# First MLP's down projection as a stream of seven block products over 16 inner tiles

## The chip, the cores and the metric

One Trainium2 chip; the program runs on one core. The metric is the device time in microseconds (us), lower is better. TensorE (PE) multiplies, VectorE (DVE), ScalarE (ACT) and GpSimd (POOL) work element by element, and SyncE (SP) issues the transfers from one queue, in which a wait holds back everything behind it.

## What is computed

Three transformer blocks follow one another on an activation x of 1024 rows and 1024 features, in 32-bit floats. The change lies in the MLP of the first block and touches that of the third:

```python
hn = rms_norm(h, norm_mlp_w)                                     # first block
h = h + jnp.square(jax.nn.relu(hn @ w_up)) @ w_down              # 1024 -> 4096 -> 1024
...
mod = jax.nn.silu(c) @ w_ada + b_ada                             # third block: 6 x 1024 values
...
h = rms_norm_3(x, norm2_pre) * (1.0 + scale2) + shift2
f = jnp.square(jax.nn.relu(h @ w_fc1)) @ w_fc2                   # 1024 -> 4096 -> 1024
x = x + gate2 * rms_norm_3(f, norm2_post)
```

`mod` needs only the input `c`, so the kernel computes it during the first block's MLP.

## The kernel before

**Precision.** Every 32-bit matmul is three: each operand is split into a rounded high part and a low part (the rest), and high x high, high x low and low x high are accumulated in PSUM. ScalarE makes the high parts (a copy into the rounded type), GpSimd or VectorE the low parts (a subtraction). A product of a 128x128 weight tile and a 128x512 half of an activation tile is thus three matmuls of 512 columns.

**Layout.** Activations are transposed: X holds 8 tiles of 128 features by 1024 rows. The 4096 hidden features are 32 inner tiles. While an MLP's up projection runs (`fast_all`, a seven-product scheme over 2x2 blocks, parts p1, p5, p6, p4, p7, p2, p3 in this order for each pair of tiles), each finished hidden tile is spilled to `hsc` in device memory, and is loaded again later.

**First MLP's down before.** 40 jobs `dn{g}_{m}`: five groups g of 8, 4, 4, 8 and 8 inner tiles, and in each group the 8 output tiles m. A job over 8 inner tiles is 48 matmuls, one over 4 is 24. Its result stands in a PSUM bank and VectorE adds it to X (`to_x`). The first three groups, jobs 0 to 23, cover inner tiles 0 to 15 with 8 x 2 x 3 x 16 = 768 matmuls. Beside the jobs VectorE forms the 48 rows of `w_ada` needed for `mod` (`row_step`, list `ADAS`): eight products of 128x128 with a column of silu(c), added up in PSUM, for each row tile; TensorE then reduces each with one short matmul (`row`, L1062) two jobs later. Their loads (`row_load`) stand in SyncE's queue.

**Third MLP's down before.** Inner tiles 0 to 23 go as a stream of seven products of blocks (`blocks`, `BLOCKS`): the output is cut in 2x2 quarters (4 output tiles by 512 rows), the inner dimension in two halves of `NK` = 12 tiles. A block takes 12 steps, one for each inner tile k of a half; a step is 4 output tiles x 3 = 12 matmuls (L842 to L844). Seven blocks do the work of eight. In the first two and the last two steps of a block TensorE takes output tiles 0 and 1 of both steps before tiles 2 and 3 (`BORDER`), so that finished banks come in two halves. For step s:

- SyncE loads weights for two steps at a time (`weight_load`, v = s // 2, four places; 512 KB for each weight block that the product needs, one or two), as soon as step 2v - 7, the last that used the place, is done, and then half tiles of the hidden activation (`block_load`, 256 KB). Quarters of it are named (half of the inner dimension, half of the rows): (0,0), (1,0), (1,1), (0,1).
- ScalarE: `block_copy(s + 1)` copies one half tile into PSUM (L1632), then `block_highs(s)` rounds the activation (L1641) and the weights (L1643) of step s.
- VectorE: adds or subtracts the second half tile where the block needs a sum, then makes the low part of step s - 1. For some steps it also adds two weight blocks. At steps 3 and 4 of the next block it adds the finished products to X (`block_out`); ScalarE does this for outputs that are written first.
- GpSimd: `block_sum(s + 1)` adds weight blocks (where VectorE doesn't), then the low part of the weights of step s.

ScalarE, VectorE and GpSimd can be at most four steps ahead of TensorE, since there are four places for the rounded activation. The order in `block_step` of ScalarE, and in that of VectorE before:

```python
if s + 1 < NSTEP:
    block_copy(s + 1)          # ScalarE
block_highs(s)
...
if sum_on_vector(s + 1):       # VectorE: s // NK == 2 or s in (3, 5, 7, 9, 11)
    tt(wblock(s + 1, 0), wblock(s + 1, 0), wblock(s + 1, 1), ADD, f"S sW {s + 1}")
block_sum(s)
block_low(s - 1)
```

The stream begins right behind the up projection. In SyncE's queue stood, before: weight load 0; then half tiles 0 to 3, weight load 1, half tiles 4 to 11, weight loads 2 and 3 (load 2 waits for the last parts of the up projection, load 3 for step 1), the spills of hidden tiles 31 and 30, and weight load 4, which waits for spill 31 to land.

The functions that the diff touches:

Of the kernel before, what the change touches and what calls it, by code (L numbers as in the profile page):

```python
# [16 lines left out]
P = 128  # L17
# [6 lines left out]
ADAS = [[0]] + [[2 * n - 1, 2 * n] for n in range(1, 9)] + [[n + 8] for n in range(9, 24)] + [[2 * n - 16, 2 * n - 15] for n in range(24, 32)] + [[]] * 8  # L24
assert sum(ADAS, []) == list(range(48))
# [19 lines left out]
NK = 12  # L45
NSTEP = len(BLOCKS) * NK
BORDER = ([(k, j) for a in (0, 2) for k in (0, 1) for j in (a, a + 1)] + [(k, j) for k in range(2, NK - 2) for j in range(4)]
          + [(k, j) for a in (0, 2) for k in (NK - 2, NK - 1) for j in (a, a + 1)])
WPLACE = [0, 1, 2, 0] + [(3, 1, 2, 0)[v % 4] for v in range(4, 36)] + [3, 1, 2, 3, 1, 2]


def sum_on_vector(s):

    return s // NK == 2 or s in (3, 5, 7, 9, 11)

# [13 lines left out]
SPLIT = ("dn0_0", "fdn0_0")  # L69
# [93 lines left out]
def stream(d):  # L163
# [13 lines left out]
    def phases(up, dn, t):  # L177
        for f in range(2 * NQ[t]):
            plan(tile_name(t, f), d[up][NQ[t] * (f % 2) + f // 2 if t == "fup" else f])
        for g, z in enumerate(SZ[t]):  # L180
            if t == "fa1_" and g < 4:
# [96 lines left out]
def build(nc, d, out):  # L278
    ctx = ExitStack()
    with ctx:  # L280
# [176 lines left out]
        AR = [T[1], RT, T[2]]  # L457
# [6 lines left out]
        BU = {(0, 0): [GF[:, k // 2, half(k % 2)] for k in range(NK)], (1, 0): [GXF[:, k // 2, half(k % 2)] for k in range(NK)],  # L464
              (1, 1): [HXF[:, k, half(1)] for k in range(4, 8)] + [HF[:, k, half(1)] for k in (4, 5, 6, 7, 0, 1, 2, 3)],
              (0, 1): [HXF[:, k, half(0)] for k in range(4, 8)] + [HF[:, k, half(0)] for k in range(4, 8)] + [HXF[:, k, half(1)] for k in range(4)]}
        wplace = (WO, TO + 4096, WO + 8192, RO)
        WF = [at(f"WF{i}", a, [P, 2048]) for i, a in enumerate(wplace)]
        WR = [at(f"WR{i}", a, [P, 2048], R) for i, a in enumerate(wplace)]
# [3748 lines left out]
```

## Time and profile before

| | us |
|---|---|
| median of 3 runs | 3313.03 (3308.84 to 3313.93) |
| profiled execution | 3316.2, its span 3314.2 |
| TensorE busy | 3255.0 |
| first MLP's down, 40 jobs | 795.73 to 1157.01 |
| of it groups 0 to 2 | 795.73 to 978.29 |
| third MLP's stream, 84 steps | 2975.72 to about 3211 |

Times in the profile count from the span's start. TensorE's matmuls overlap: the length given for one (389 ns for 512 columns) is longer than the distance to the next. The clock column is TensorE's granted clock, 1.00 being 2.4 GHz and 0.50 being 1.2 GHz.

### The profile page before, as it was taken

Reading aid. Unit: us, or ns where it says so; the run is one execution under the profiler, and the core shown is the slowest. Engines: PE = TensorE matmul, PEld = TensorE weight load, DVE = VectorE, ACT = ScalarE, POOL = GpSimd, SP = SyncE. Lnnn points to the kernel's source line nnn. Section 1 sums busy time; section 2 is a strip of 40 time slices with the busy share of each in tenths; the row PEclk is TensorE's granted clock in tenths of the full one; section 3 lists DMA queues with packets and bytes.
Section 4 is the critical chain, followed back from the end, with each engine's and each line's share of the span. In section 5 each row is a group of like instructions: output and inputs, shape, how many; then the busy total and the mean of one; then the engine's idle time right before and its main releaser. Section 6 shows DMA issues by size and latency. Waiting matters only on the chain.

```text
span 3314.2 us, 40211 instructions
## 1 busy us (share of the span) xinstructions
PE 3255.0 (98%) x16118; PEld 2648.4 (80%) x16118; DVE 2008.5 (61%) x2966; ACT 1299.0 (39%) x2014; POOL 1288.5 (39%) x768
## 2 busy tenths in 40 slices
PE   8999999999999999998999999999999999999998
PEld 6788888888888878875687888888888888887887
DVE  4563347665564538577558888776536485655553
ACT  5332233333121221176535545521223364456652
POOL 3112324555353213231424554554212215555963
PEclk9999999999999999999999999999999999999999
DMA  3011312235554212111022222366111132247743
GB/s 111 31 58 65 127 51 96 110 117 191 177 206 165 96 39 70 57 66 42 5 98 70 77 82 90 107 230 231 58 59 45 39 133 108 110 158 241 238 149 121
DMA packets 142502, 358.36 MB, mean 108 GB/s; under 512 B 15958, under 2 KB 58726, under 8 KB 142188
## 3 DMA queue, kind: packets, MB, share of 16 engines
q1 hardware_dynamic: 142316, 355.79, 30.8%
q8 instruction: 128, 2.10, 0.3%
q14 instruction: 58, 0.48, 0.1%
HBM read 292.66 MB, written 63.09 MB: 107 GB/s over the span
## 4 chain that ended last, share of the span: by engine, by line
PE 90%; DVE 5%; ACT 2%; DMA 1%; POOL 1%; issue 0%; SPq 0%; POOLq 0%; DVEq 0%; ACTq 0%
PE ps L751 16%; PE ps L752 16%; PE ps L754 16%; PE ps L809 9%; PE ps L811 9%; PE ps L810 9%; PE ps L842 2%; PE ps L843 2%; PE ps L844 2%; PE ps L993 1%; PE ps L1216 1%; PE ps L784 1%; PE ps L786 1%; PE ps L785 1%; PE ps L1265 1%; PE ps L1249 1%
## 5 line engine op out<-in xcount | busy, mean ns | idle before, releaser
L3512 POOL TENSOR_TENSOR wlo<-raw,whi 128x1024 fp32r<-128x1024 f32 (+3 forms) x162 | 388.6, 2399 | 1174.8 <-ACT whi L1499 1174.8
L751 PE MATMUL ps<-HH,whi 128*128 128x512 f32 (+2 forms) x1520 | 607.1, 399 | 2.3 <-DVE HL L2358 1.4
L752 PE MATMUL ps<-HL,whi 128*128 128x512 f32 (+2 forms) x1520 | 597.1, 393 | 0.0
L1499 ACT ACTIVATE whi<-raw 128x1024 fp32r<-128x1024 f32 (+3 forms) x164 | 163.2, 996 | 817.3 <-PE ps L754 789.6
L754 PE MATMUL ps<-HH,wlo 128*128 128x512 f32 (+2 forms) x1536 | 476.6, 392 | 0.0
L3582 POOL TENSOR_TENSOR wlo<-raw,whi 128x512 fp32r<-128x512 f32 x188 | 275.0, 1464 | 281.4 <-ACT whi L1596 240.2
L754 PEld LDWEIGHTS ps<-HH,wlo 128*128 128x128 f32 (+2 forms) x1536 | 287.3, 187 | 66.0 <-issue 1.1
L751 PEld LDWEIGHTS ps<-HH,whi 128*128 128x128 f32 (+2 forms) x1520 | 285.0, 188 | 67.0 <-issue 3.0
L752 PEld LDWEIGHTS ps<-HL,whi 128*128 128x128 f32 (+2 forms) x1520 | 284.9, 187 | 61.9 <-issue 2.0
L2342 DVE TENSOR_TENSOR T<-T,ps 128x512 f32<-128x512 f32 (+1 forms) x254 | 174.3, 699 | 231.1 <-PE ps L811 192.4
L2342 DVE TENSOR_TENSOR X<-ps,X 128x1024 f32<-128x1024 f32 (+1 forms) x91 | 108.1, 1188 | 313.9 <-PE ps L754 296.8
L751 PE MATMUL ps<-GH,whi 128*128 128x512 f32 x752 | 295.8, 393 | 0.8 <-POOL wlo L3512 0.6
L809 PE MATMUL ps<-OHp,whi 128*128 128x512 f32 x752 | 292.7, 389 | 0.9 <-POOL wlo L3582 0.9
L752 PE MATMUL ps<-GL,whi 128*128 128x512 f32 x752 | 292.8, 389 | 0.0
L810 PE MATMUL ps<-OLp,whi 128*128 128x512 f32 x752 | 292.6, 389 | 0.0
L754 PE MATMUL ps<-GH,wlo 128*128 128x512 f32 x784 | 241.6, 389 | 0.0
L809 PE MATMUL ps<-HH,whi 128*128 128x512 f32 x564 | 219.6, 389 | 1.6 <-POOL wlo L3582 1.6
L810 PE MATMUL ps<-HL,whi 128*128 128x512 f32 x564 | 219.4, 389 | 0.0
L1596 ACT ACTIVATE whi<-raw 128x512 fp32r<-128x512 f32 x188 | 118.0, 628 | 193.4 <-PE ps L811 187.9
L754 PEld LDWEIGHTS ps<-GH,wlo 128*128 128x128 f32 x784 | 147.2, 188 | 31.1
L3582 POOL TENSOR_TENSOR HH<-HXF,whi 128x512 fp32r<-128x512 f32 x93 | 121.9, 1311 | 113.6 <-ACT whi L1596 60.1
L809 PEld LDWEIGHTS ps<-OHp,whi 128*128 128x128 f32 x752 | 141.2, 188 | 30.8 <-POOL wlo L3582 1.6
(514 smaller groups left out, 6624.8 us busy)
## 6 DMA issues: line engine op xcount, KB each, us to landing
raw<-in_w_up SPq DMA_DIRECT2D x76, 512.0 KB, 4.1
WF<-in_w_fc SPq DMA_DIRECT2D x72, 512.0 KB, 4.5
raw<-in_w_in SPq DMA_DIRECT2D x62, 512.0 KB, 3.3
hsc<-T SPq DMA_DIRECT2D x62, 512.0 KB, 2.7
GF<-hsc SPq DMA_DIRECT2D x42, 512.0 KB, 5.8
raw<-in_w_down SPq DMA_DIRECT2D x40, 512.0 KB, 5.3
raw<-in_w_fc SPq DMA_DIRECT2D x40, 512.0 KB, 4.0
T<-in_w_ada SPq DMA_DIRECT2D x32, 512.0 KB, 3.8
```

Of the source, the lines that this page charges most:

```text
L751: e.matmul(o_[0:m, half(hf)], whi_[k], hi[k0 + k][:, half(hf)], start=first, stop=False)
L752: e.matmul(o_[0:m, half(hf)], whi_[k], lo[k0 + k][:, half(hf)], start=False, stop=False)
L754: i = e.matmul(o_[0:m, half(hf)], wlo_[k], hi[k0 + k][:, half(hf)], start=False, stop=last)
L809: e.matmul(bank[p], wh[:, blk(k)], hi, start=k == 0 and p not in ("p2", "p7", "p3"), stop=False, skip_group_check=True)
L810: e.matmul(bank[p], wh[:, blk(k)], lo, start=False, stop=False, skip_group_check=True)
L811: i = e.matmul(bank[p], wl_[:, blk(k)], hi, start=False, stop=k == 3, skip_group_check=True)
L842: e.matmul(o_, wh, hi, start=k == 0, stop=False, skip_group_check=True)
L1499: e.activation(whi_of(name), v3(raw_of(name), 2) if name in SPLIT else raw_of(name), ACT.Copy).then_inc(*ac.inc("hi " + name))
L1596: e.activation(wh_of(t, w), part(t, n, p)[0], ACT.Copy).then_inc(*ac.inc(f"{t}hi {n} {p}"))
L2342: e.tensor_tensor(o, a, b, op).then_inc(*dv.inc(*names))
L3512: e.tensor_tensor(wlo_of(name), raw_of(name), whi_of(name).bitcast(F), SUB).then_inc(*po.inc("lo " + name))
L3582: e.tensor_tensor(o, x, wh_of(t, w).bitcast(F), SUB).then_inc(*po.inc(f"{t}lo {n} {p}"))
```

## The change

The first MLP's inner tiles 0 to 15 go as a stream too: seven blocks of 8 steps, 672 matmuls, in place of jobs 0 to 23. Jobs 24 to 39 (groups 3 and 4) stay; job 24 takes its inner tiles in the order 4 to 7, 0 to 3. `NK`, `NSTEP`, `BORDER`, `WPLACE` become tables by MLP ("up" is the first, "fa1_" the third); the first has a fifth weight place. Its stream order in SyncE's queue is `blocks1`: quarter (1,0) from weight load 5 on, (1,1) from 9 on, (0,1) from 21 on. In it all outputs are added to X by VectorE. A weight place is two separate halves.

In both streams VectorE adds the weight blocks of every odd step above 4 in blocks that have two, and does so after the low part of step s - 1 and not before the sum of step s. At the stream's start weight loads 1, 2, 3 stand behind half tiles 1, 3 and 5. In the third MLP half tiles 8 to 11 of quarter (0,0) come behind weight loads 3 and 4, quarter (1,0) comes with weight loads 7 to 12 (before: 3 to 8) and quarter (1,1) with 13 to 18 (before: 9 to 14).

The 48 rows become 12 groups of four (`ROWQ`), formed at jobs 24 to 32, 34, 36 and 38: eight products of 512 columns each, from four tiles of 512 KB (from group 9 on two tiles are free, and the second half of a group is loaded when the first has been used). The up projection takes its PSUM banks in the same order in both MLPs.

```diff
-ADAS = [[0]] + [[2 * n - 1, 2 * n] for n in range(1, 9)] + [[n + 8] for n in range(9, 24)] + [[2 * n - 16, 2 * n - 15] for n in range(24, 32)] + [[]] * 8
+ROWQ = {24 + n: n for n in range(9)} | {34: 9, 36: 10, 38: 11}
...
-NK = 12
+NK = {"up": 8, "fa1_": 12}
+G0 = {"up": 3, "fa1_": 4, "fup": 0}
+WPLACE = {"up": [0, 4, 2, 0] + [(1, 3, 2, 0)[v % 4] for v in range(4, 27)] + [1],
+          "fa1_": [0, 1, 2, 0] + [(3, 1, 2, 0)[v % 4] for v in range(4, 36)] + [3, 1, 2, 3, 1, 2]}
...
-def sum_on_vector(s):
-    return s // NK == 2 or s in (3, 5, 7, 9, 11)
+def sum_on_vector(t, s):
+    b = s // NK[t]
+    return BLOCKS[b][1] is not None and s % 2 == 1 and s > 4
...
             fast_all("up")
-            for n in range(40):
+            blocks("up")
+            for n in range(24, 40):
...
-            def block_step(s):
-                if sum_on_vector(s + 1):
-                    q.wait_ge(*wload_of(s + 1))
-                    tt(wblock(s + 1, 0), wblock(s + 1, 0), wblock(s + 1, 1), ADD, f"S sW {s + 1}")
-                if s < NSTEP:
-                    block_sum(s)
+            def block_step(t, s):
+                if s < NSTEP[t]:
+                    block_sum(t, s)
                 if s:
-                    block_low(s - 1)
-                if s > NK and s % NK in (3, 4):
-                    block_out(s // NK - 1, s % NK - 3)
+                    block_low(t, s - 1)
+                if s + 1 < NSTEP[t] and sum_on_vector(t, s + 1):
+                    q.wait_ge(*wload_of(t, s + 1))
+                    tt(wblock(t, s + 1, 0), wblock(t, s + 1, 0), wblock(t, s + 1, 1), ADD if BLOCKS[(s + 1) // NK[t]][2] > 0 else SUB, f"{t}S sW {s + 1}")
+                if s > NK[t] and s % NK[t] in (3, 4):
+                    block_out(t, s // NK[t] - 1, s % NK[t] - 3)
...
+            def blocks1():
+                for v in range(3, NSTEP["up"] // 2):
+                    if v == 27:
+                        loads(widx["dn3_1"])
+                    if v > 3:
+                        weight_load("up", v)
+                    for k in (2 * (v - 5) % 8, 2 * (v - 5) % 8 + 1):
+                        if 4 < v < 9:
+                            block_load("up", 1, 0, k, pe("up15 p4"))
+                        elif 8 < v < 13:
+                            block_load("up", 1, 1, k, pe("up15 p7"))
+                        elif 20 < v < 25:
+                            block_load("up", 0, 1, k, pe("upS 3"))
...
-                    for k in (2 * (v - 3) % NK, 2 * (v - 3) % NK + 1):
-                        if v < 9:
-                            block_load(1, 0, k, pe("fa1_15 p7"), ac(f"S cp {k}"))
-                        elif v < 15:
-                            block_load(1, 1, k, pe("fa1_15 p3"), dv(f"S sT {NK + k}"), *([spilled("fa1_", 30)] if k > 9 else []))
+                    if v in (3, 4):
+                        for k in (2 * v + 2, 2 * v + 3):
+                            block_load("fa1_", 0, 0, k, pe("fa1_15 p6"))
+                    for k in (2 * (v - 7) % 12, 2 * (v - 7) % 12 + 1):
+                        if 6 < v < 13:
+                            block_load("fa1_", 1, 0, k, pe("fa1_15 p7"), ac(f"fa1_S cp {k}"))
+                        elif 12 < v < 19:
+                            block_load("fa1_", 1, 1, k, pe("fa1_15 p3"), dv(f"fa1_S sT {12 + k}"), *([spilled("fa1_", 30)] if k > 9 else []))
...
-                    if (t, n) == ("fa1_", z):
-                        for k in range(4):
-                            block_load(0, 0, k, pe("fa1_15 p5"))
-                        weight_load(1)
-                        for k in range(4, NK):
-                            block_load(0, 0, k, pe("fa1_15 p5" if k < 8 else "fa1_15 p6"))
-                        weight_load(2)
-                        weight_load(3)
+                    if t in NK and n == z:
+                        for k in range(8):
+                            block_load(t, 0, 0, k, pe(f"{t}15 p5"))
+                            if k in (1, 3, 5):
+                                weight_load(t, (k + 1) // 2)
```

## Rows read from the trace of the kernel before

**Rows 1.** The page: busy time of the engines, and one costly group of VectorE.
```profile
PE 3255.0 (98%) x16118; PEld 2648.4 (80%) x16118; DVE 2008.5 (61%) x2966; ACT 1299.0 (39%) x2014; POOL 1288.5 (39%) x768
...
L2342 DVE TENSOR_TENSOR T<-T,ps 128x512 f32<-128x512 f32 (+1 forms) x254 | 174.3, 699 | 231.1 <-PE ps L811 192.4
```

**Rows 2.** Timeline of TensorE, first matmuls of stream blocks 1 and 2 (start, length).
```profile
3014.37 0.39 PE L842 MATMUL ps<-HH,WR 128*128 128x512 f32 x1
...
3047.01 0.39 PE L842 MATMUL ps<-HH,WR 128*128 128x512 f32 x1
```

**Rows 3.** Timeline of TensorE, first MLP's down: start, end of group 2, end.
```profile
795.73 0.39 PE L751 MATMUL ps<-GH,HH 128*128 128x512 f32 x1
...
978.15 0.28 PE L1062 MATMUL ps<-ones,adat 128*128 128x1 f32 x2
...
978.29 0.48 PE L751 MATMUL ps<-HH,whi 128*128 128x512 f32 x1
...
1157.01 0.39 PE L751 MATMUL ps<-HH,whi 128*128 128x512 f32 x1
```

**Rows 4.** Timeline of TensorE, third MLP's stream; bracketed: idle time and its end.
```profile
2975.72 0.39 PE L842 MATMUL ps<-HH,WR 128*128 128x512 f32 x1
...
2985.42 0.47 PE L842 MATMUL ps<-HH,WR 128*128 128x512 f32 x1 [1.22 <-POOL WR L3518]
...
2999.05 0.47 PE L842 MATMUL ps<-HH,WR 128*128 128x512 f32 x1 [2.44 <-POOL WR L3518]
...
3003.48 0.39 PE L842 MATMUL ps<-HH,WR 128*128 128x512 f32 x1
...
3050.36 0.47 PE L842 MATMUL ps<-HH,WR 128*128 128x512 f32 x1 [0.46 <-ACT ps L1632]
```

**Rows 5.** Windows: length, busy time by engine, granted clock, DMA share, GB/s.
```profile
2999.00:3003.40 4.40, 4.36 (x12) 3.47 (x13) 1.48 (x3) 2.75 (x6) 3.71 (x3) 0.61 1.00 358
...
3145.60:3178.20 32.60, 32.60 (x145) 27.00 (x145) 23.95 (x35) 23.51 (x42) 29.60 (x21) 1.00 0.78 266
```

**Rows 6.** Timeline of SyncE's queue, the last spills of the third MLP.
```profile
2982.47 0.50 SPq L3744 DMA_DIRECT2D hsc<-T  x1
...
2984.21 0.53 SPq L3744 DMA_DIRECT2D hsc<-HF  x1
```

**Rows 7.** DMA issues, windows from 2982.4, 2984.1, 3014.5, 3041.7, 3124: us to landing.
```profile
hsc<-T SPq DMA_DIRECT2D x1, 512.0 KB, 6.5
...
hsc<-HF SPq DMA_DIRECT2D x1, 512.0 KB, 5.9
...
HXF<-hsc SPq DMA_DIRECT2D x2, 256.0 KB, 4.4
...
HF<-hsc SPq DMA_DIRECT2D x2, 256.0 KB, 5.3
...
HF<-hsc SPq DMA_DIRECT2D x2, 256.0 KB, 6.4
```

**Rows 8.** Timeline of SyncE's queue, two weight loads in block 1.
```profile
3041.76 0.94 SPq L3744 DMA_DIRECT2D WF<-in_w_fc  x2
```

**Rows 9.** Timelines of ScalarE (copy) and GpSimd (low part), third MLP's block 1.
```profile
3045.42 0.60 ACT L1632 ACTIVATE ps<-HXF 128x512 f32<-128x512 f32 x1 [0.36 <-DVE HL L2342]
...
3047.17 1.30 POOL L3518 TENSOR_TENSOR WR<-WF,WR 128x512 fp32r<-128x512 f32 x1 [0.74 <-ACT WR L1643]
```

**Rows 10.** Timelines of GpSimd and VectorE, weight sums that met the other's work.
```profile
2982.24 1.81 POOL L3518 TENSOR_TENSOR WF<-WF 128x512 f32<-128x512 f32 x1 [3.53 <-DMA WF<-in_w_fc]
...
3047.32 1.70 DVE L2342 TENSOR_TENSOR WF<-WF 128x512 f32<-128x512 f32 x1 [1.99 <-DMA WF<-in_w_fc]
```

**Rows 11.** Timeline of VectorE, outputs of block 4 into X.
```profile
3145.80 2.47 DVE L2342 TENSOR_TENSOR X<-X,ps 128x512 f32<-128x512 f32 x4
```

**Rows 12.** Timeline of VectorE, norm low parts at the end of the first MLP.
```profile
1147.59 3.42 DVE L2358 SCALAR_TENSOR_TENSOR HL<-X,gprod,HH 128x1024 fp32r<-128x1024 f32 x1
...
1162.12 1.28 DVE L2358 SCALAR_TENSOR_TENSOR HL<-X,gprod,HH 128x1024 fp32r<-128x1024 f32 x1
```

More of the change, by code:

```diff
@@ L1064, in row_step @@
             def row_step(n):
-                for f in rows.pop(0):
-                    if f == 0:
-                        q.wait_ge(*ac("n2 rt"))
-                    q.wait_ge(*dv(f"red ada{f}"))
-                    row(f)
-                rows.append(ADAS[n] if n >= 0 else [])
+                for g in rows.pop(0):
+                    for f in range(4 * g, 4 * g + 4):
+                        q.wait_ge(*dv(f"red ada{f}"))
+                        row(f)
+                rows.append([ROWQ[n]] if n in ROWQ else [])
             def norm2(k):
@@ L2319, in scalar @@
             fast_all("fa1_", bias7)
-            for s in range(4, NSTEP):
-                block_step(s)
             for n in range(32, 40):
@@ L3606, in fast_all @@
                 for w in range(m):
-                    if w == m - 3 and t != "fa1_":
+                    if w == m - 3 and t not in NK:
                         lows(following(t, -1))
                     fast_lo(t, w)
-                if t == "fa1_":
-                    block_sum(0)
-                    for s in range(NSTEP):
-                        block_step(s)
+                if t in NK:
+                    block_sum(t, 0)
+                    for s in range(NSTEP[t]):
+                        block_step(t, s)
                     return
@@ L3631, in gpsimd @@
             fast_all("up")
-            for n in range(40):
+            for k in (0, 2):
+                low(f"dnl {16 + k}", GXF[:, k, :], HH[:, k, :], HL[:, k, :], ac(f"dnh {16 + k}"))
+            for n in range(24, 40):
                 down("up", n)
@@ L3872, in blocks @@
-            def blocks():
-                for v in range(3, NSTEP // 2):
+                f = k + NK[t] * l
+                q.wait_ge(*spilled(t, f))
+                load(f"hr{k}", BU[t][l, h][k], hsc[f][:, half(h)], f"{t}S{l}{h} {k}")
+            def blocks1():
[11 more added lines that the diff above has]
+                            block_load("up", 0, 1, k, pe("upS 3"))
+                    if 12 < v < 17:
+                        k = v - 9
+                        q.wait_ge(*pe("up15 p3"))
+                        q.wait_ge(*spilled("up", 16 + k))
+                        load(f"hr{8 + k}", HF[:, k, :], hsc[16 + k], f"uphr {16 + k}")
+                    elif v > 23:
+                        k = v - 24
+                        q.wait_ge(*dv(f"upS sT {4 * NK['up'] - 1}"))
+                        q.wait_ge(*spilled("up", 16 + k))
+                        load(f"hr{8 + k}", GXF[:, k, :], hsc[16 + k], f"uphr {16 + k}")
@@ L3875, in blocks, with blocks3 @@
+            def blocks3():
+                for v in range(3, NSTEP["fa1_"] // 2):
                     if v == 41:
```

433 lines of the change are left out of this document (238 added, 195 removed).

## The prediction, made before the changed kernel was run

> **What bounds the kernel now.** The page first. TensorE is busy for 98% of the span [rows 1]. So two things can move the time: how many matmuls there are, and how long TensorE stands still or runs slowly between them. The page's mean of a matmul, 389 ns, is not its price, because matmuls overlap. The timeline gives the price: block 1 of the third MLP's stream is 144 matmuls from 3014.37 to 3047.01 us, so 0.2267 us each [rows 2]. A step of a stream (one inner tile, 12 matmuls) is then 2.72 us and a block of eight steps 21.8 us.
>
> Next the stage that is replaced. The first MLP's down runs from 795.73 to 1157.01, and its first 24 tiles, 768 matmuls, end at 978.29 [rows 3]. They take 182.6 us, of which 768 x 0.2267 = 174.1 are matmuls; the remaining 8.5 are the 30 rows of the modulation vector that are reduced there, about 0.25 us each (0.14 to the next matmul, 978.15 to 978.29, which is itself 0.09 longer [rows 3]), and 1 us of short gaps.
>
> Then the stage that already works in the new way. The third MLP's stream starts at 2975.72. It has three stalls: 1.22 us of idle before 2985.42 and 2.44 before 2999.05, both until GpSimd had made a low part of weights, and 0.46 before 3050.36 [rows 4]. After the second TensorE's granted clock is 0.61 of full in 2999.0 to 3003.4, a mix of 1.2 and 2.4 GHz [rows 5]: 12 matmuls take 3003.48 - 2999.05 = 4.43 us for 2.72, so the drop costs 1.7 us [rows 4]. The idle of 1.22 us had none. The end of block 4 shows none: 32.60 busy of 32.60 us [rows 5].
>
> **The change, part by part.**
> (1) Fewer matmuls. 7 blocks x 8 steps x 12 = 672 for 768: 96 x 0.2267 = 21.8 us off. The 1 us of gaps goes too. The 48 rows stay, four at a time, at the same price. Gain 22.8.
>
> (2) The start of the new stream. Count from its first matmul; step n starts at 2.72 n. In a block's first and last two steps output tiles 0 and 1 come first, so a block's last step begins half a step early: step 7 needs its operands at 6.5 x 2.72 = 17.7. The queue waits for step 1 (5.4), then issues two weight loads, two half tiles (now put behind them) and the last two spills, by about 8.1. It then waits for spill 30 before weight load 4. In the third MLP spill 30 was issued at 2984.21 and took 5.9 us, to 2990.1, 14.4 after its stream's start; spill 31, of 0.5 MB like it, landed 1.1 us before, at 2988.97 [rows 6, 7]. Here 0.5 MB more is ahead, so 1.1 us, but the spill is issued a little earlier: I take 15. Then come two single loads and the first half tile of quarter (1,0), issued at 16.1; such a tile lands in 4.4 us behind one weight load [rows 7], 5 behind two: 21. VectorE sums that tile for step 8 before it makes the low part of step 7 (0.70 us each [rows 1]), so step 7 starts at 22.4: 4.7 us late. Bounds: 2 (the spill too lands in 4.4) and 7 (two more transfers' worth of queue).
>
> (3) The tiles of quarter (1,1), and of (0,1) in the first MLP, are now loaded four steps ahead. The pair for steps 2v-2 and 2v-1 is issued once step 2v-7 is done, behind two weight loads. ScalarE copies tile 2v-2 BEFORE it rounds tile and weights of step 2v-3, so step 2v-3 is behind the transfer. From the end of 2v-7 to the start of 2v-3 there are three steps, 8.2 us. The chain: the first weight load is issued at 3041.76, two steps before 3047.01 and so 0.2 after the end of its step, the second is out at 3042.70 and the tile follows [rows 2, 8], 1.2; landing 5.3 (median of that pair [rows 7]), 6.5; copy, rounding, rounding and GpSimd's low part, 3045.42 to 3048.47 [rows 9], 3.1. With the hand-off it is 9.6, so 1.4 us of stall. For the pair that opens a block, step 2v-3 is the last of the block before and begins half a step early: 2.8. A stall delays the next pair's loads just as much, so only every second pair adds one. Block 2 of the first MLP: 2.8 + 1.4 = 4.2. Block 5, whose (0,1) is copied in the same way: 4.2. Block 2 of the third, six pairs: 2.8 + 1.4 + 1.4 = 5.6, where before the loads were issued eight steps earlier and only the 0.6 at 3050.36 was lost: 5.0 net. Quarter (1,0) goes through VectorE and is behind a single weight load: 0.6 + 4.4 + 1.5 = 6.5 us, in time. Together 13.4; bounds 0 (landing under 3.9 us) and 21 (landing 6.4 us, as one pair did [rows 7], 1.1 us for each of the seven stalls).
>
> (4) The third MLP's start. Weight load 2 no longer stands behind twelve half tiles, so the 1.22 us goes. But load 4 decides, and it waits for spill 31, issued at 2982.47 and landed 6.5 us later [rows 6, 7]; two half tiles are now ahead of it, 1.1 us. 1.1 later in all; bounds -3 (2999.05's stall goes) and +3.
>
> (5) The clock. Four stalls here are of about 2.6 us or more (the start, the two openings of block 2, that of block 5), as long as the 2.44 that was followed by half speed. I charge 1.7 us for three of them: 5.1. Bounds 0 and 7. The Trainium skill (TensorE: Matmul & The Clock Gate, The HAM clock gate) says that the full clock is granted to activity and withdrawn for its lack; by that rule all four would be charged, 6.8.
>
> (6) Weight sums. Every second one goes to VectorE, in the third MLP 28 of 60 for 17. GpSimd had two operations of 1.3 us in a step of 2.72 [rows 9] and kept up, so nothing is gained at TensorE. A sum met by a GpSimd operation costs both: GpSimd 1.81 for 1.30 [rows 9, 10], VectorE 1.70 for 0.70 [rows 1, 10]. Two steps of GpSimd are then at most 3 x 1.3 + 0.5 = 4.4 of 5.44. The new order on VectorE (low part before the sum) removes a wait behind a weight load. 0; bounds -0.6 and the first rival. The Trainium skill (SBUF — State Buffer, SBUF: two separate sides) calls the pair of ports these engines share a lock held for the whole instruction; rows 10 agree, and the sum stays.
>
> (7) Block ends. VectorE alone adds the products into X here, at worst four half tiles in 2.47 us after each half of a block [rows 11]. The bank that they free is wanted one step into the next block; in the third MLP block 4 has this worst case and TensorE does not wait [rows 5]. 0.
>
> (8) Rows beside groups 3 and 4. Per tile VectorE has 1.2 us for X and eight products of 512 wide, about 0.65 each: 6.4 of 11.8. From row group 9 only two tiles are free, so half of each group is loaded while VectorE waits, some 4 us. In tile 38 that makes 9.5, and the two following norm operations, one of which takes 3.42 beside GpSimd [rows 12], end 2.7 to 4.7 us into what was idle time. The last low part was done at 1163.4, 6.4 after the last down tile [rows 3, 12]; gg0 needs it at 9.5. 1.0; bounds 0 and 4.
>
> **Sum.** -22.8 + 4.7 + 13.4 + 1.1 + 5.1 + 1.0 = +2.5 us on the profiled execution (3316.2 us, span 3314.2). The median of the runs shown is 3313.0; from it I get 3315.5, so 3316.
>
> **The rivals.** 0.2% is 6.6 us; less cannot be told from no change here.
> A, as summed, within 6.6 us either way: 0.44.
> B, slower: VectorE becomes the bound of the first MLP's stream. Point of decision: 21.8 us of work in a block of eight. It has sixteen tile operations at a spacing of 2.47 / 4 = 0.62 us [rows 11], 9.9; outputs 4.9; four weight sums at 0.70, 2.8, or at 1.70, 6.8. That is 17.6 or 21.6, before any hand-off between it and ScalarE. If the hand-offs add 1.7 us to the latter, 1.5 us is lost in each of six blocks, 9 us in all; with the charges of A, 2.5, it is 3325. For it: VectorE reads two SBUF operands while GpSimd works for more than half of the time. Against: at the worst block end of the third MLP nothing waited, though no weight sum lay there. 0.27 with larger stalls in (2) and (3).
> C, faster: the transfers are hidden. If the tiles of (3) land in under 3.9 us, or the engines run further ahead than I think, (3) and two clock charges go: -22.8 + 4.7 + 1.7 + 1.1 + 1.0 = -14.3, 3299. For it: behind one weight load a tile lands in 4.4. Against: behind two it took 5.3 and 6.4 [rows 7]. If half of the gain comes, 3306. 0.29.
>
> **How the numbers follow.** Faster 0.29, same 0.44, slower 0.27. A alone is 3306 to 3320. The range runs from C's full gain, 3299, to B with one more clock charge, 3328.
>
> **What would show it.** In the changed profile: 672 matmuls on the block lines before the first MLP's last two groups; a stall of about 5 us near step 7 there, ended by VectorE's low part behind a landing of GXF; in both streams, at the end of block 1 and at step 3 of block 2, idle of 1 to 3 us ended by GpSimd's low part, with ScalarE's copy waiting for a transfer; stretches at 1.2 GHz behind them; no stall in the last 16 down tiles. Wrong would be: copies that never wait for transfers (C), or VectorE without idle time from one block end to the next (B).

## The result and the profile after

The changed kernel takes 3323.93 us (median of 6 runs, 3318.79 to 3326.22). The kernel before, run beside it, takes 3311.51 (6 runs, 3305.77 to 3313.93). The ratio is 1.0035, with a 95% interval of 1.0023 to 1.0047: slower by 12 us. That is inside the predicted range of 3299 to 3328 and 8 above the predicted 3316. The profiled execution took 3323.6 us, its span is 3321.8. That is 7.6 more than the span before. The profiled execution before was itself 4.7 us above the median of its runs, so 7.6 and 12 don't contradict each other.

The page of the changed kernel, busy time of the engines:

```profile
PE 3246.0 (98%) x16022; PEld 2633.1 (79%) x16022; DVE 2058.9 (62%) x2839; ACT 1354.8 (41%) x2142; POOL 1302.3 (39%) x795
```

The 96 matmuls are gone (16118 in [rows 1], 16022 here) and yet the time is longer. TensorE's timeline in the first MLP's stream (start, length; in brackets the idle time ahead and what ended it):

```profile
794.85 0.39 PE L855 MATMUL ps<-HH,WR 128*128 128x512 f32 x1
...
810.23 0.47 PE L855 MATMUL ps<-HH,WR 128*128 128x512 f32 x1 [1.60 <-POOL WR L3547]
...
818.23 0.80 PE L855 MATMUL ps<-HH,WR 128*128 128x512 f32 x1 [3.63 <-DVE HL L2357]
...
845.50 0.47 PE L855 MATMUL ps<-HH,WR 128*128 128x512 f32 x1 [2.65 <-POOL WR L3547]
...
853.19 0.47 PE L855 MATMUL ps<-HH,WR 128*128 128x512 f32 x1 [0.63 <-DVE X L2357]
...
917.17 0.47 PE L855 MATMUL ps<-HH,WR 128*128 128x512 f32 x1 [2.38 <-POOL WR L3547]
...
925.69 0.47 PE L855 MATMUL ps<-HH,WR 128*128 128x512 f32 x1 [1.31 <-DVE X L2357]
...
949.28 0.47 PE L855 MATMUL ps<-HH,WR 128*128 128x512 f32 x1 [0.87 <-DVE HL L2357]
...
969.80 0.39 PE L764 MATMUL ps<-HH,whi 128*128 128x512 f32 x1
```

The stream takes 969.80 - 794.85 = 174.95 us. Its 672 matmuls at 0.2267 are 152.3, so 22.6 are lost. In the text below a stall is the delay of the next matmul against 0.2267 us of spacing; it is some 0.15 longer than the idle time in the bracket (1.75 for 1.60). The losses by place: 1.75 and 3.79 at the start and 2.5 of half speed behind them; 2.82 and 2.54 at the last step of blocks 1 and 4, where blocks 2 and 5 are about to open; 7.3 in eleven smaller stalls (0.79, 0.43, 0.52, 0.62, 0.80, 1.47, 0.43, 0.28, 0.30, 0.61, 1.03), seven of them ended by VectorE, two by GpSimd and two too short for a name; 1.9 in gaps too small to list. The 16 tiles behind it, with all 48 rows, run from 969.80 to 1155.32. From its start to there the first MLP's down takes 360.5 us, where it took 361.3 from its start to the same point [rows 3]. So of the 22.8 us that the missing matmuls and gaps were to give, 22.6 are lost again inside the stream.

TensorE's timeline in the third MLP's stream:

```profile
2974.16 0.39 PE L855 MATMUL ps<-HH,WR 128*128 128x512 f32 x1
...
2986.64 0.47 PE L855 MATMUL ps<-HH,WR 128*128 128x512 f32 x1 [1.44 <-POOL WR L3547]
...
2997.63 0.51 PE L855 MATMUL ps<-HH,WR 128*128 128x512 f32 x1 [2.55 <-POOL WR L3547]
...
3016.98 0.47 PE L855 MATMUL ps<-HH,WR 128*128 128x512 f32 x1 [1.14 <-DVE X L2725]
...
3045.88 0.76 PE L855 MATMUL ps<-HH,WR 128*128 128x512 f32 x1 [2.71 <-POOL WR L3547]
...
3061.02 0.47 PE L855 MATMUL ps<-HH,WR 128*128 128x512 f32 x1 [1.09 <-POOL WR L3547]
...
3218.51 0.39 PE L764 MATMUL ps<-GH,whi 128*128 128x512 f32 x1
```

That is 244.35 us, where the kernel before took 235.2 (2975.72 [rows 4] to 3210.94): 9.1 more. Where block 2 opens there was a stall of 0.6 [rows 4]; now there is one of 2.87 at the last step of block 1 (3045.88) and, at steps 3 and 7 of block 2, 1.25 and 1.20. The stalls at the start are nearly those of before. A stall of 1.30 one step into block 1 (3016.98) is new: TensorE wants a bank of block 0 back, whose output VectorE writes (line 2725). The two traces agree elsewhere: the first stream starts 0.9 us earlier, the first MLP's down is 0.8 shorter, from there to the third stream it is 0.1 longer, and behind the third stream it is the same. -0.9 - 0.8 + 0.1 + 9.1 is 7.5, the 7.6 of the span within rounding.

How the first stream starts, on SyncE's queue:

```profile
802.49 0.91 SPq L3781 DMA_DIRECT2D hsc<-T  x2
810.24 0.94 SPq L3781 DMA_DIRECT2D WF<-in_w_down  x2
811.22 0.97 SPq L3781 DMA_DIRECT2D GXF<-hsc  x2
```

and on VectorE:

```profile
816.88 0.70 DVE L2357 TENSOR_TENSOR ps<-GXF,ps 128x512 f32<-128x512 f32 x1 [5.65 <-DMA GXF<-hsc]
817.49 0.68 DVE L2357 TENSOR_TENSOR HL<-ps,HH 128x512 fp32r<-128x512 f32 x1
```

The last spills go out at 802.49 and land 6.9 us later. Weight load 4 follows at 810.24, the half tiles of (1,0) stand behind it, and VectorE waits 5.65 us for the first before it makes the low part that TensorE needs at 818.23. This is the mechanism of step (2) of the prediction; TensorE starts 23.4 us behind the stream's start, where 22.4 was expected.

How block 2 opens there. SyncE's queue, ScalarE (copy, rounding of tile, rounding of weights) and GpSimd:

```profile
836.02 0.94 SPq L3781 DMA_DIRECT2D WF<-in_w_down  x2
837.00 0.98 SPq L3781 DMA_DIRECT2D GXF<-hsc  x2
```

```profile
842.37 0.60 ACT L1648 ACTIVATE ps<-GXF 128x512 f32<-128x512 f32 x1 [2.66 <-DMA GXF<-hsc]
842.91 0.58 ACT L1657 ACTIVATE HH<-ps 128x512 fp32r<-128x512 f32 x1
843.39 0.62 ACT L1659 ACTIVATE WR<-WF 128x512 fp32r<-128x512 f32 x1
...
847.65 0.60 ACT L1648 ACTIVATE ps<-GXF 128x512 f32<-128x512 f32 x1 [1.60 <-DMA GXF<-hsc]
```

```profile
844.08 1.27 POOL L3547 TENSOR_TENSOR WR<-WF,WR 128x512 fp32r<-128x512 f32 x1 [1.75 <-ACT WR L1659]
```

From the first weight load to TensorE are 845.50 - 836.02 = 9.5 us; the prediction had 9.6. And what the prediction did not follow, VectorE in the same place:

```profile
844.20 1.70 DVE L2357 TENSOR_TENSOR WF<-WF,WF 128x512 f32<-128x512 f32 x1
...
848.91 0.69 DVE L2357 TENSOR_TENSOR HL<-ps,HH 128x512 fp32r<-128x512 f32 x1 [2.24 <-ACT HH L1657]
849.52 1.73 DVE L2357 TENSOR_TENSOR WF<-WF,WF 128x512 f32<-128x512 f32 x1
851.17 0.68 DVE L2357 TENSOR_TENSOR HL<-ps,HH 128x512 fp32r<-128x512 f32 x1
851.77 2.47 DVE L2357 TENSOR_TENSOR X<-ps,X 128x512 f32<-128x512 f32 x4
```

The outputs of block 1 (851.77) free a bank that TensorE wants. They stand in VectorE's order behind the low part of 848.91, which waits 2.24 us for ScalarE, which waits at 847.65 for the next late tile; and behind a weight sum of 1.73. TensorE waits for them at 853.19.

TensorE's clock behind five stalls (windows: length, PE busy, granted clock, DMA share, GB/s):

```profile
818.80:824.20 5.40, 5.40 (x15) 0.55 0.06 20
845.50:849.70 4.20, 4.20 (x19) 1.00 0.50 176
917.20:921.30 4.10, 4.10 (x18) 1.00 0.58 201
2997.60:3002.00 4.40, 4.37 (x12) 0.61 0.56 194
3045.90:3050.00 4.10, 4.10 (x12) 0.61 0.49 172
```

### The profile page after: what moved, and what is told of

It is laid out like the page before. It is cut to its first block, busy times and chain, and to the rows that moved or that the text cites. A ratio compares the mean times of both kernels' runs of the same rounds, so it can differ in the third digit from the quotient of the medians.

```text
span 3321.8 us, 40243 instructions
## 1 busy us (share of the span) xinstructions
PE 3246.0 (98%) x16022; PEld 2633.1 (79%) x16022; DVE 2058.9 (62%) x2839; ACT 1354.8 (41%) x2142; POOL 1302.3 (39%) x795
## 4 chain that ended last, share of the span: by engine, by line
PE 88%; DVE 6%; ACT 2%; DMA 2%; POOL 1%; issue 1%; SPq 0%; POOLq 0%; DVEq 0%; ACTq 0%
PE ps L764 14%; PE ps L765 14%; PE ps L767 14%; PE ps L822 9%; PE ps L824 9%; PE ps L823 9%; PE ps L855 3%; PE ps L857 3%; PE ps L856 3%; PE ps L1007 1%; PE ps L1230 1%; PE ps L797 1%; PE ps L799 1%; PE ps L798 1%; PE ps L1279 1%
## 5 line engine op out<-in xcount | busy, mean ns | idle before, releaser
L3541 POOL TENSOR_TENSOR wlo<-raw,whi 128x1024 fp32r<-128x1024 f32 (+3 forms) x139 | 353.3, 2542 | 1081.0 <-ACT whi L1515 1081.0
L764 PE MATMUL ps<-HH,whi 128*128 128x512 f32 (+2 forms) x1456 | 581.1, 399 | 2.3 <-DVE HL L2373 1.4
L767 PE MATMUL ps<-HH,wlo 128*128 128x512 f32 (+1 forms) x1472 | 457.5, 392 | 0.0
L767 PEld LDWEIGHTS ps<-HH,wlo 128*128 128x128 f32 (+1 forms) x1472 | 275.1, 187 | 63.2 <-issue 1.1
L2357 DVE TENSOR_TENSOR T<-T,ps 128x512 f32<-128x512 f32 (+1 forms) x254 | 174.2, 699 | 228.8 <-PE ps L824 190.0
L855 PE MATMUL ps<-HH,WR 128*128 128x512 f32 x560 | 222.7, 398 | 25.9 <-POOL WR L3547 16.6
L3547 POOL TENSOR_TENSOR WR<-WF,WR 128x512 fp32r<-128x512 f32 x140 | 191.2, 1369 | 137.1 <-ACT WR L1659 137.0
L2357 DVE TENSOR_TENSOR X<-ps,X 128x512 f32<-128x512 f32 (+1 forms) x135 | 121.5, 924 | 194.6 <-PE ps L767 170.5
L764 PE MATMUL ps<-GH,whi 128*128 128x512 f32 x576 | 226.1, 393 | 0.6 <-POOL wlo L3541 0.6
L765 PE MATMUL ps<-GL,whi 128*128 128x512 f32 x576 | 224.2, 389 | 0.0
L857 PE MATMUL ps<-HH,WR 128*128 128x512 f32 x560 | 220.3, 393 | 0.0
L856 PE MATMUL ps<-HL,WR 128*128 128x512 f32 x560 | 220.2, 393 | 0.0
```

Source lines behind the costliest of these rows:

```text
L764: e.matmul(o_[0:m, half(hf)], whi_[k], hi[k0 + k][:, half(hf)], start=first, stop=False)
L765: e.matmul(o_[0:m, half(hf)], whi_[k], lo[k0 + k][:, half(hf)], start=False, stop=False)
L767: i = e.matmul(o_[0:m, half(hf)], wlo_[k], hi[k0 + k][:, half(hf)], start=False, stop=last)
L855: e.matmul(o_, wh, hi, start=k == 0, stop=False, skip_group_check=True)
L856: e.matmul(o_, wh, lo, start=False, stop=False, skip_group_check=True)
L857: i_ = e.matmul(o_, wl_, hi, start=False, stop=k == NK[t] - 1, skip_group_check=True)
```

## The experiments

The totals of the twelve kernels move with the other 2,900 us too: the first stream began anywhere between 789.3 and 799.0 us in them. So each is read by the length of the two streams in its trace, with the ratio of its time to the kernel before as a check. A stream's length goes from its first matmul to the first one of what follows; there is one trace of each kernel. Where two kernels have the same code for a stream, it differs by up to 0.7 us in the first MLP (e3 and e6) and by up to 1.9 in the third (243.3 to 245.2 in the kernels with the changed one's loads), so differences of that size are no effect by themselves. Theory 1 is the prediction's: late transfers, with ScalarE's copy queued ahead of its roundings. Theory 2: VectorE, with weight sums and all outputs, is what the stream waits for.

| run | first stream | third stream | median us | ratio to before (95%) |
|---|---|---|---|---|
| before | none | 235.2 | 3311.5 | 1 |
| after | 175.0 | 244.4 | 3323.9 | 1.0035 (1.0023 to 1.0047) |
| e1 | 174.2 | 233.1 | 3311.4 | 0.9998 (0.9989 to 1.0008) |
| e2 | 171.2 | 240.7 | 3314.9 | 1.0005 (0.9996 to 1.0015) |
| e3 | 162.3 | 243.9 | 3310.1 | 0.9990 (0.9980 to 1.0000) |
| e4 | 172.1 | 243.9 | 3319.2 | 1.0022 (1.0012 to 1.0031) |
| e5 | 168.6 | 243.3 | 3318.5 | 1.0020 (1.0010 to 1.0030) |
| e6 | 161.6 | 234.5 | 3297.3 | 0.9967 (0.9954 to 0.9979) |
| e7 | 154.4 | 232.2 | 3286.7 | 0.9932 (0.9919 to 0.9946) |
| e8 | 161.1 | 231.8 | 3298.5 | 0.9970 (0.9959 to 0.9982) |
| e9 | 153.3 | 231.9 | 3286.3 | 0.9929 (0.9915 to 0.9942) |
| e10 | 155.2 | 233.1 | 3288.3 | 0.9937 (0.9923 to 0.9952) |
| e11 | 161.5 | 245.2 | 3309.2 | 0.9993 (0.9982 to 1.0003) |
| e12 | 153.6 | 231.9 | 3287.8 | 0.9934 (0.9920 to 0.9948) |

Some of the expectations below give lengths 0.2 to 0.5 us shorter than this table (161.8 for e3's first stream); they were read from or to a neighbouring matmul. The kernel before was run again beside each group of kernels (medians 3311.5, 3310.8, 3308.6 and 3311.9), and each ratio is against its own group.

**e1, the third MLP's loads as they were.**

```diff
-if v in (3, 4): ... block_load("fa1_", 0, 0, k, ...)
-for k in (2 * (v - 7) % 12, 2 * (v - 7) % 12 + 1):
-    if 6 < v < 13:    block_load("fa1_", 1, 0, k, ...)
-    elif 12 < v < 19: block_load("fa1_", 1, 1, k, ...)
+for k in (2 * (v - 3) % 12, 2 * (v - 3) % 12 + 1):
+    if v < 9:    block_load("fa1_", 1, 0, k, ...)
+    elif v < 15: block_load("fa1_", 1, 1, k, ...)
...
+if (t, n) == ("fa1_", z):   # all twelve half tiles of (0,0) first, as in the kernel before
+    for k in range(12):
+        block_load(t, 0, 0, k, ...)
+        if k == 3:
+            weight_load(t, 1)
+    weight_load(t, 2)
+    weight_load(t, 3)
```

> The changed kernel, with the loads of the third MLP's stream in the order of the kernel before (its quarters (1,0) and (1,1) from step pair 3 and 9 on, four pairs earlier, and all twelve half tiles of (0,0) ahead of weight load 2). The changed kernel's third stream took 244.3 us, 235.4 before. Theory 1 (late transfers in front of ScalarE's copy): the stalls of 2.87, 1.25 and 1.20 us at the opening of block 2 and behind it go, with one clock charge, and the third stream takes 236 to 238 us; the whole is 6 to 8 us shorter than the changed kernel's. Theory 2 (VectorE, which now makes every second weight sum, is late): the order of loads changes little, and the stream stays above 241 us, with stalls ended by VectorE's low parts.

The third stream took 233.05 us, 11.3 less than in the changed kernel and 2 less than before. All stalls beyond the start are gone; these two are all that is left of it:

```profile
2979.60 0.47 PE L855 MATMUL ps<-HH,WR 128*128 128x512 f32 x1 [1.61 <-POOL WR L3547]
...
2992.93 0.47 PE L855 MATMUL ps<-HH,WR 128*128 128x512 f32 x1 [2.19 <-POOL WR L3547]
```

Theory 1 holds here, and theory 2 falls: VectorE has the same sums as in the changed kernel, and TensorE never waits for it in this stream. Even the 1.30 us one step into block 1 went, though it had been ended by VectorE. In the changed kernel VectorE had waited 2.19 us for a half tile of quarter (1,0) just ahead of that output (at 3012.66, and 6.07 us at 3007.23); in e1 it waits for no transfer there. The gain is larger than the 6 to 8 us expected: this stall was not in the sum, and the 2.19 us of idle was not followed by half speed this time (its window is shown at the end).

**e2, ScalarE's order turned round in both streams.**

```diff
-if s + 1 < NSTEP[t]:
-    block_copy(t, s + 1)
 block_highs(t, s)
+if s + 1 < NSTEP[t]:
+    block_copy(t, s + 1)
```

> The changed kernel, but ScalarE rounds tile and weights of a step before it copies the tile of the next one, in both streams; the loads stand where they were. Theory 1: the transfer then has one step (2.72 us) more, so the stalls ended by GpSimd's low part at the end of block 1 (2.82 us) and of block 4 (2.54 us) of the first MLP and of block 1 of the third (2.87 us, and 1.25 and 1.20 behind it) go: some 10 us of idle and a clock charge or two, if the later copy itself makes no new wait for VectorE's sum. Theory 2 (VectorE late): those stalls stay or turn into waits for VectorE, and the total stays within 3 us of the changed kernel's, or above it, since VectorE gets its copied tile later.

3.8 us came back in the first stream and 3.6 in the third: less than theory 1 expected. The stalls at the two starts grew, from 3.79 to 4.46 and from 2.71 to 3.55 us. The stall ended by GpSimd where block 2 opens is down to 0.58 in the first MLP and 0.81 in the third, and that of block 5 is gone (1.33 there is ended by VectorE's low part), so the order on ScalarE was indeed what joined them to the transfer. But TensorE now waits for the outputs: 7.7 us in nine stalls of the first stream, where it was 3.1 in four. TensorE and VectorE, same place:

```profile
849.06 0.47 PE L855 MATMUL ps<-HH,WR 128*128 128x512 f32 x1 [1.36 <-DVE X L2357]
```

```profile
847.03 0.69 DVE L2357 TENSOR_TENSOR HL<-ps,HH 128x512 fp32r<-128x512 f32 x1 [2.81 <-ACT HH L1657]
847.63 2.47 DVE L2357 TENSOR_TENSOR X<-ps,X 128x512 f32<-128x512 f32 x4
```

VectorE has no weight sum between the two, and still the outputs come late, by the 2.81 us that the low part before them waits for ScalarE's rounding, which stands behind a copy that waited 2.78 us for the same transfer. The late tile reaches TensorE by two ways: through the operands, and through the outputs that stand behind its low part. e2 closes one of them.

**e3 and e11, the first MLP's quarters (1,1) and (0,1) earlier.** e3 loads them four steps earlier, eight ahead of their use; e11 (run later) six ahead.

```diff
 if 4 < v < 9:
     block_load("up", 1, 0, k, pe("up15 p4"))
-elif 8 < v < 13:  block_load("up", 1, 1, k, pe("up15 p7"))
-elif 20 < v < 25: block_load("up", 0, 1, k, pe("upS 3"))
+if 6 < v < 11:    block_load("up", 1, 1, (k - 4) % 8, ...)   # e11: 7 < v < 12, (k + 2) % 8
+elif 16 < v < 21: block_load("up", 0, 1, k, pe("upS 3"))     # e11: 19 < v < 24, (k + 2) % 8
```

> The changed kernel, with the quarters (1,1) and (0,1) of the first MLP's stream loaded earlier: (1,1) in step pairs 7 to 10 instead of 9 to 12, (0,1) in 17 to 20 instead of 21 to 24. The first stream takes 175.0 us in the changed kernel, of which 152.3 are matmuls. Theory 1: the stalls of 2.82 and 2.54 us go and the smaller ones of VectorE just behind (0.79 + 0.43 and 1.47 + 0.43, caused by the late copies) shrink: 6 to 8 us less, 167 to 169. Theory 2: the stalls of 2.82 and 2.54 go but VectorE's part stays, 3 us and more in blocks 2 and 5: about 170. If the loads have nothing to do with it: 175.

> The changed kernel, with quarters (1,1) and (0,1) of the first MLP's stream loaded one step pair earlier, six steps ahead instead of four (e3: eight). By the prediction's chain the step that is held needs 9.6 us from the issue of the weight load, and has 8.2 with four steps of lead and 13.6 with six: so six are enough, and the stream takes 162 to 164 us, as in e3 (161.8). If the queue or the landing were much slower than the chain says (over 13 us), stalls would stay and the stream would be near 168.

162.3 us and 161.5: 13 us less, where 6 to 8 were expected of e3. TensorE's group of the line that leads each step, over the stream (busy, mean ns, then idle time ahead and what ended it), in the changed kernel:

```profile
L855 PE MATMUL ps<-HH,WR 128*128 128x512 f32 x224 | 89.8, 401 | 15.8 <-POOL WR L3547 7.5 <-DVE HL L2357 5.5 <-DVE X L2357 2.5
```

and in e11:

```profile
L855 PE MATMUL ps<-HH,WR 128*128 128x512 f32 x224 | 88.0, 393 | 6.6 <-DVE HL L2357 3.6 <-POOL WR L3547 3.0
```

The waits for X are all gone, and of those for a low part of VectorE only the 3.6 of the start is left. So the small stalls of VectorE behind the openings were consequences of the late transfers too. (e3 has two of 0.47 and 0.28 in block 1.) That six steps do what eight do fits the chain of 9.6 us: it has 8.2 with four steps of lead and 13.6 with six. In e11 the third MLP, whose loads were left late, lost its time as in the changed kernel (245.2). What stays in the first stream beside the start is one stall of 1.4 to 1.5 us at the last step of block 1. In e3, VectorE on the tiles of block 1:

```profile
811.28 0.69 DVE L2357 TENSOR_TENSOR ps<-GXF,ps 128x512 f32<-128x512 f32 x1 [5.51 <-DMA GXF<-hsc]
...
823.44 0.69 DVE L2357 TENSOR_TENSOR ps<-GXF,ps 128x512 f32<-128x512 f32 x1 [2.61 <-DMA GXF<-hsc]
...
831.16 0.70 DVE L2357 TENSOR_TENSOR ps<-GXF,ps 128x512 f32<-128x512 f32 x1 [2.85 <-DMA GXF<-hsc]
```

VectorE waits for quarter (1,0), which the prediction called "in time", at three of the four pairs of block 1. That this is what leaves the stall of 1.5 us is argued here; e7 bears on it.

**e4, the first MLP's weight sums all on GpSimd.** The edit makes `sum_on_vector` false for "up".

> The changed kernel, with all weight sums of the first MLP's stream back on GpSimd (VectorE keeps those of the third). Theory 1: the 0.79 + 0.43 and 1.47 + 0.43 us behind the block ends and the single 0.3 to 1.0 us ended by VectorE's low part shrink, as VectorE gets 1.7 us in every second step back, while the 2.82 and 2.54 stay: 172 to 174 us for the stream of 175.0. Theory 2 (VectorE is the bound of the stream): 5 us and more come back, under 170. If GpSimd can't keep up with two operations of 1.3 to 1.8 us in each step of 2.72, the stream gets longer, with stalls ended by GpSimd's low part all over blocks 0, 2, 3, 4 and 5.

172.1 us: 2.8 came back, as theory 1 had it. The stalls for X fell from 0.79 and 1.47 to 0.65 and 0.67, the openings stayed (2.50, 2.64), and two ended by GpSimd (1.08, 0.82) stand behind block 2's opening where there had been 0.52, 0.62 and 0.80. With late tiles the sums on VectorE cost 3 us; they are not the bound.

**e5, the start.** Four half tiles of (1,0) ahead of weight load 4.

```diff
+if v == 4:
+    for k in (0, 1, 2, 3):
+        block_load("up", 1, 0, k, pe("up15 p4"), bload_of("up", 0, 0, k))
 if v > 3:
     weight_load("up", v)
...
-if 4 < v < 9:
+if 6 < v < 9:
     block_load("up", 1, 0, k, pe("up15 p4"))
```

> The changed kernel, but the first four half tiles of quarter (1,0) are issued ahead of weight load 4 (which waits for spill 30) and of weight load 5, instead of behind them. Theory 1 (the start is held by the queue: spill 30, weight loads, then the half tile that VectorE sums): the 3.79 us stall at 23.4 us of the first stream and the half speed behind it (2.5 us) go: the stream of 175.0 takes 169 to 171. Rival (weight load 4 itself, waiting for spill 30, decides the same step): the stall stays above 2 us, now ended by GpSimd's low part, and the stream stays above 173.

168.6 us, 6.4 less: the 3.79 us and the half speed behind them are gone (3.8 + 2.5 = 6.3), and nothing took their place. The opening of block 2 fell from 2.82 to 2.30, and the other stalls moved by 0.4 at most.

**e6, e3 and e1 together.**

> The load orders of e1 (third MLP) and of e3 (first MLP) together. The two streams are 2,100 us apart, so by every theory they add: 162 us for the first stream and 233 for the third, where the changed kernel took 175.0 and 244.3. Against the kernel before: the first MLP's down is shorter by 22.8 less the 9.5 us that its stream loses and 1 beside the rows, 12; the third stream by 2; so 3313 - 14 = 3299 us, ratio 0.996.

161.6 and 234.5, ratio 0.9967. The effects add (3297.3 us, 3299 expected), and the change as a whole turns from 0.35% slower to 0.33% faster with nothing altered but the order of loads.

**e7, and quarter (1,0) and the third MLP's start.** On top of e6: e5's edit with the other four tiles of (1,0) at v = 5 and 6, and the third stream's places of weights in the order of the first, so that load 4 takes a place free after step 3.

```diff
-"fa1_": [0, 1, 2, 0] + [(3, 1, 2, 0)[v % 4] for v in range(4, 36)] + [3, 1, 2, 3, 1, 2]
+"fa1_": [0, 1, 2, 0] + [(1, 3, 2, 0)[v % 4] for v in range(4, 36)] + [1, 3, 2, 1, 3, 2]
```

> As e6, with quarter (1,0) of the first MLP's stream also two step pairs earlier and ahead of weight load 4, and with the third stream's weight load 4 put into a buffer that is free after step 3, where it waited for the last spill (load 5 takes the buffer that waits for it). Theory 1: the first stream loses its stall of 3.68 us with the slow clock behind it and the 1.47 at 48.8 us: 156 to 158 us of 161.8. The third loses the 2.34 us at 23.3: 231 of 233. So about 7 us under e6. Rival: the weight load behind spill 30 takes over in the first stream, and it stays above 160.

The first stream takes 154.35 us, 7.2 less than in e6 and below the 156 to 158 expected, with a single stall; TensorE there:

```profile
796.47 0.39 PE L855 MATMUL ps<-HH,WR 128*128 128x512 f32 x1
...
811.83 0.47 PE L855 MATMUL ps<-HH,WR 128*128 128x512 f32 x1 [1.59 <-POOL WR L3547]
...
950.82 0.39 PE L764 MATMUL ps<-HH,whi 128*128 128x512 f32 x1
```

The stall of 1.5 us at the last step of block 1 is gone with the earlier (1,0); this run took away the start's stall too, so what (1,0) alone is worth there is not separated. The third stream gained 2.3 against e6, but its second stall did not go: 2.44 became 1.58 us, and the rest of the gain is the slow clock behind it, which e1 had escaped with the old places (233.1). Against the kernel before the ratio is 0.9932: 22 us faster.

**e8 and e10, weight sums as before, on top of e6 and of e7.** `sum_on_vector` is false in the first MLP, and in the third true in block 2 and steps 3, 5, 7, 9 and 11.

> As e6, but with the weight sums where the kernel before has them: all on GpSimd in the first MLP's stream, and in the third on VectorE only in block 2 and in steps 3, 5, 7, 9 and 11. If moving sums to VectorE is worth nothing at TensorE (my term of 0): within 2 us of e6 in each stream (162 and 233), at most 235 in the third as in the kernel before. If GpSimd with two operations in every step of 2.72 us can't keep up, stalls ended by its low part appear in the blocks with two weight quarters and the streams are 3 us longer or more. If VectorE is the tighter engine, the first stream gets shorter, under 160.

> As e7, with the weight sums placed as in the kernel before (e8's edit). e8 against e6 gave 0.7 us in the first stream and 2.9 in the third for sums on GpSimd, both within what a stall at the start makes. If VectorE's sums cost TensorE something wherever the operands are late: the third stream takes 230 to 231 us of 232.2, the first 154 as before. If nothing is late any more and the sums are free: no difference over 0.5 us in either.

e8: 161.1 and 231.8 for e6's 161.6 and 234.5. The 2.7 us in the third are nearly all at its start (its second stall there is 0.90 for 2.44, without half speed), and e6 had itself 1.4 more than e1 with the same loads and sums, by the half speed behind that stall. e10: 155.2 and 233.1 for e7's 154.4 and 232.2. So with tiles in time it makes no difference over 0.9 us who adds the weights; the two ratios, 0.9937 and 0.9932, can't be told apart. Neither branch of e10's expectation was met: not 230 to 231 us, and not a difference of 0.5 at most.

**e9 and e12, what stays at the start.** e9: in the first MLP weight load 3, which waits for step 1, goes behind half tiles 6 and 7 of (0,0). e12: e9 and e10 together.

```diff
-if k in (1, 3, 5):
-    weight_load(t, (k + 1) // 2)
+if k in (1, 3, 7):
+    weight_load(t, (1, 3, 7).index(k) + 1)
```

> As e7, with weight load 3 of the first MLP's stream issued behind the last two half tiles of quarter (0,0), which it held until step 1 was done. Theory: the stall of 1.74 us before step 5.5 (ScalarE waited 2.98 us for such a half tile) goes, and the stream of 154.35 us takes 152.5 to 153. Rival: weight load 3, now later, becomes the wait of step 6, and the stream stays at 154 or above.

> e9 and e10 together: all loads early, weight load 3 behind the half tiles, weight sums as in the kernel before. If both are worth what was expected of each: first stream 152.5 to 153, third 230 to 231, and the whole 2 to 3 us under e7 (ratio to the kernel before 0.9932): 0.992 to 0.993.

e9's first stream takes 153.3 us, 1.0 over its matmuls; the stall of 1.75 is 0.68. e12 takes 153.6. Both lie a little above the 152.5 to 153 expected. In the third stream both have about 232, where 230 to 231 was expected of e12, and its total is that of e7 and e9 within the error. The best kernels (e7, e9, e12) are 0.66 to 0.71% faster than before, 22 to 24 us, and 1.0% faster than the change as made.

## Why the prediction was nearly right, and where it was not

The likeliest case was "as summed, within 6.6 us", 3306 to 3320. Measured is 12 us slower, 4 above that and near the number of rival B, but not by B's mechanism. On the profiled execution the sum gave +2.5 us and 7.6 was measured. That the miss is no larger is in part luck: 7.3 us of stalls priced at nothing met terms that were too high (2.8 in (3), 1.1 in (5), 0.9 in (2)). By its own steps:

- **(1) Matmuls.** Right: 672 for 768.
- **(2) The start, 4.7.** The mechanism was right in every link (half tile expected out 16.1 us after the stream's start, it went at 16.4; step 7 expected 22.4 after, it began at 23.4), and e5 shows it. Size 3.79 for 4.7; and a stall of 1.75 ahead of it, which was not foreseen. e9 removes 1.1 of that by taking weight load 3 from in front of the last half tiles of (0,0).
- **(3) Tiles four steps ahead, 13.4.** The openings were put at 2.8 us three times and measured 2.82, 2.54 and 2.87; the later pairs of the third MLP at 1.4 twice, measured 1.25 and 1.20. e1, e3 and e11 show the cause. The 1.4 us put on a later pair in each of blocks 2 and 5 of the first MLP did not come as such: what delay there was lies in the small stalls of (7). One part was wrong: "Quarter (1,0) goes through VectorE ... in time". VectorE waited for it at three of four pairs of block 1 in e3 and at five of six in the third MLP's block 1 of the changed kernel, and in e7, with it earlier, the last 1.5 us stall was gone.
- **(4) The third MLP's start, +1.1.** Wrong in its reasons, small in size. The 1.22 us "goes" because weight load 2 is earlier, it said; the stall stayed, at 1.60. In the changed trace ScalarE spends 2979.23 to 2983.6 on four bias and square passes of the up projection before the rounding that step 4 needs. It had waited 1.99 us for a half tile just ahead of them; in e1 no copy ahead of the same four passes waits for a transfer, and the stall is 1.77. That the passes cause it is argued from these traces, not tried.
- **(5) Clock, 5.1.** Three of the four stalls were charged 1.7. Two paid: 2.5 behind the start, 1.5 behind 3045.88. (The one behind 2997.63 was there before the change too.) Behind the openings of blocks 2 and 5 in the first MLP the clock stayed at 1.00. Total 4.0.
- **(6) Weight sums, 0.** Right where the tiles are in time, to 0.9 us (e10 against e7). With late tiles they cost 2.8 us (e4).
- **(7) Block ends, 0. This is the step that failed.** It took the margin from a stream of the kernel before in which no tile was late [rows 5, 11], and (3) had just said that tiles would be late. VectorE's outputs stand behind its low part, and that behind ScalarE's wait for the tile. So the late tiles of blocks 2 and 5 were paid twice: at the operands, and in stalls of 0.79, 0.43, 1.47 and 0.43 for X, 3.1 us. Another 4.2 follow in seven small stalls, of which (3) had priced 2.8 as its later pairs; that they come from the lead of the engines being used up is argued. e11 shows what is behind all eleven: with the tiles six steps ahead all 7.3 went, sums and outputs being the same, and in e3 too behind the openings. e2 shows the second way by itself. The stall of 1.30 in the third MLP is the same step: an output behind VectorE's and ScalarE's wait for a tile of (1,0), gone in e1.
- **(8) Rows.** 1.0 expected. The 16 tiles with 48 rows ran as long as their parts, and the tail costs 0.8: from 1155.32 to the norm's sums at 1166.98 are 11.7 us, where it was 10.9 (1157.01 [rows 3] to 1167.89). Of this 0.7 came back before the third stream; where stays open.

The sum of the first stream's terms was 4.7 + 8.4 and two clock charges, 16.5 us, against 22.6 measured. The difference, 6.1, is the 7.3 of small stalls, 1.75 at the start and 1.9 of small gaps, less the terms that were too high. In the third stream 7.8 stands against 9.1; the stall of 1.30 one step into block 1, for which (7) had 0, is as large as the gap between them, though the other terms missed by up to 0.8 either way. The upper end of the range, 3328, is not what its words give: B's 3325 with one more clock charge of 1.7 is 3327, and the measured time is below either.

**The rivals.** B (VectorE is the bound) is wrong as a mechanism: e4 takes the sums away for 2.8 us, e11 leaves them and gains 13.5. Its count of VectorE's work, 17.6 to 21.6 of 21.8 us, leaves little to catch up with, which fits that late tiles cost more than their stalls. C (transfers hidden) is wrong: ScalarE's copy waits 2.66 and 1.60 us for them. Its price, -14 us, is near what e6 gave when the loads were made early (ratio 0.9967, -11 us).

## What to carry to other kernels

Where a stream has several engines in fixed orders, a late transfer is charged at every queue that stands behind it. Price the operand's stall, and then look at what else the waiting engine, and the one that waits for it, have behind: outputs, bank releases. A margin read from a stretch where nothing was late says nothing about one where something is. And a transfer's lead is the whole chain to the consumer (9.6 us here: two weight loads ahead of it, landing, copy, roundings, low part), in steps of TensorE, plus the half step by which a block's border moves an order forward: six steps of 2.72 us did all that eight did, and with four the stream lost 13 us.

## What the hardware showed that was not expected

The clock after a stall is not told by its length. In the changed kernel idle times of 2.65 and 2.38 us left the granted clock at 1.00, and 2.55 and 2.71 were followed by 0.61 (the windows above). In e5 the longer of two stalls of the third stream, 2.74 us of idle before 2994.10, kept it, and the shorter, 2.31 before 3040.53, did not:

```profile
2994.10:2998.30 4.20, 4.20 (x19) 1.00 0.53 181
3040.60:3044.80 4.20, 4.20 (x12) 0.59 0.55 190
```

Two stalls of the same 2.19 us of idle, at the same place of the third stream, in e1:

```profile
2992.90:2997.10 4.20, 4.17 (x18) 1.00 1.06 375
```

and in e3:

```profile
2978.00:2982.20 4.20, 4.20 (x12) 0.59 0.59 205
```

One kept 2.4 GHz, one ran partly at 1.2. What decides between them stays open. The Trainium skill (TensorE: Matmul & The Clock Gate, The HAM clock gate) has the full clock withdrawn for lack of activity. The prediction drew from this that four stalls of the changed kernel would be charged, 6.8 us, which is more than the page says of such stalls; two were, 4.0 us. For a forecast from these traces it is a charge of 1.5 to 2.5 us with a chance, not a charge for each stall.
